# Block 1: six gate tiles of each input projection multiplied inside the attention, and the keys over 512 turned in a second pass

## The reference, cut to what matters

```python
h  = modulate(rms_norm(x,  norm1_g[l]), sh1, sc1)       # latent, 512 tokens
hc = modulate(rms_norm(xc, norm1_g[l]), csh1, csc1)     # context, 256 tokens
qa, ka, va, qb, kb, vb, ga, gb = split_in_proj(h @ w_in[l])
qac, kac, vac, qbc, kbc, vbc, gac, gbc = split_in_proj(hc @ w_in[l])
ya = window_attention_latent(...)   # 128 near keys each way + 256 context keys, with a sink
yb = full_attention_latent(...)     # all 512 + 256 = 768 keys
m  = sigmoid(ga) * (ya @ w_pa) + sigmoid(gb) * (yb @ w_pb)
x  = x + gt1 * (m @ w_o)
```

## Time and profile before

| | |
|---|---|
| median of 3 runs | 3453.82 us (3453.39 to 3454.66) |
| the profiled execution | 3448.93 us |
| its span, first to last instruction | 3447.0 us |
| PE busy | 3302.1 us, 96% |
| DVE, ACT, POOL busy | 51%, 35%, 13% |
| mean granted clock of PE | 0.991 |

### The profile page before, as it was taken

The page is one execution under the profiler, slowest core; times in us unless marked ns, Lnnn a source line. Parts: engine busy times, 40 slices in busy tenths (PEclk is TensorE's granted clock), DMA queues, the critical chain, the costliest instruction groups (busy, mean ns, idle before and its releaser), DMA issues. The chain is left out here.

```text
span 3447.0 us, 49601 instructions
## 1 busy us (share of the span) xinstructions
PE 3302.1 (96%) x20432; PEld 2649.0 (77%) x20432; DVE 1772.4 (51%) x2736; ACT 1203.7 (35%) x2054; POOL 446.6 (13%) x477
## 2 busy tenths in 40 slices
PE   6999999999999999999999999999999998899998
PEld 4887778788888787776887877667888777578886
DVE  5875657664232456655323357654443385744433
ACT  3214762321131222763223333353332333532322
POOL 0211112000000021104500133120000022200000
PEclk9999999999999999999999999999999999999999
DMA  6420013354111121012222221012222220122222
GB/s 243 147 99 19 2 56 135 135 183 141 62 68 68 58 83 68 2 50 93 94 92 97 99 86 56 26 49 92 92 94 103 98 86 3 38 91 92 98 98 80
DMA packets 78265, 290.66 MB, mean 84 GB/s; under 512 B 8672, under 2 KB 9056, under 8 KB 77280
## 3 DMA queue, kind: packets, MB, share of 16 engines
q1 hardware_dynamic: 78048, 287.55, 23.6%
HBM read 285.42 MB, written 2.10 MB: 83 GB/s over the span
## 5 line engine op out<-in xcount | busy, mean ns | idle before, releaser
L459 DVE TENSOR_TENSOR w_low<-ring,w_high 128x1024 fp32r<-128x1024 f32 x418 | 526.9, 1261 | 1348.9 <-ACT w_high L456 1348.2
L494 PE MATMUL ps<-arena_r,w_high 128*128 128x512 f32 x3568 | 1146.1, 386 | 11.2 <-PEq L1517 9.2
L456 ACT ACTIVATE w_high<-ring 128x1024 fp32r<-128x1024 f32 x418 | 442.8, 1060 | 1516.0 <-PE ps L494 1506.9
L494 PEld LDWEIGHTS ps<-arena_r,w_high 128*128 128x128 f32 x3568 | 647.4, 188 | 162.8 <-issue 14.1
L494 PE MATMUL ps<-low,w_high 128*128 128x512 f32 (+1 forms) x2448 | 764.1, 361 | 0.0
L494 PE MATMUL ps<-high,w_high 128*128 128x512 f32 x2368 | 736.4, 361 | 16.2 <-DVE low L992 8.1
L494 PE MATMUL ps<-high,w_low 128*128 128x512 f32 x2368 | 730.8, 359 | 0.0
L494 PE MATMUL ps<-arena_r,w_low 128*128 128x512 f32 (+1 forms) x1456 | 546.5, 388 | 0.0
L494 PEld LDWEIGHTS ps<-high,w_high 128*128 128x128 f32 x2368 | 394.9, 188 | 96.4 <-issue 12.2
L494 PEld LDWEIGHTS ps<-low,w_high 128*128 128x128 f32 x2448 | 411.4, 189 | 74.6 <-issue 0.2
L494 PEld LDWEIGHTS ps<-high,w_low 128*128 128x128 f32 x2368 | 394.9, 188 | 70.4 <-issue 1.0
(11 more groups left out here) (353 smaller groups left out, 2902.5 us busy)
## 6 DMA issues: line engine op xcount, KB each, us to landing
ring<-in_weights SPq DMA_DIRECT2D x428, 512.0 KB, 3.2
arena<-in_ada_rows SPq DMA_DIRECT2D x80, 512.0 KB, 3.9
arena<-in_ada SPq DMA_DIRECT2D x16, 512.0 KB, 15.5
arena<-in_cond_rows SPq DMA_DIRECT2D x3, 1024.0 KB, 5.5
xL<-in_x SPq DMA_DIRECT2D x1, 2048.0 KB, 9.8
out<-xL SPq DMA_DIRECT2D x4, 512.0 KB, 2.7
low_f<-in_low_rank SPq DMA_DIRECT2D x3, 512.0 KB, 4.3
const<-in_const SPq DMA_DIRECT2D x1, 1104.0 KB, 5.2
```

The costliest lines, as they stand in the source:

```text
L456: act.activation(w_high[:, slot, :], ring[:, place, :], ACT.Copy).then_inc(unit_high.sem, 1)
L459: dve.tensor_tensor(w_low[:, slot, :], ring[:, place, :], w_high[:, slot, :].bitcast(F32), ALU.subtract).then_inc(unit_free.sem, 1)
L494: mm = pe.matmul(bank(4 * (t % 2) + 2 * p + s, width), w, g.split[k][s][x], start=(n == 0 and m == 0), stop=(n == len(part) - 1 and m == 2))
```

## The change

Of the 28 tiles of each input projection the last six (gates) are no longer multiplied for the latent tokens there. In layer 0 a third gemm makes these six tiles for the 256 context columns alone; their units come a second time in the weight stream. In both layers a new class `LateGates` multiplies the latent part inside the attention: one tile takes four steps, six of its 24 products in each step, three after the turn and three after the values, from step 1 to step 24, into bank 6. DVE evicts a tile at the next tile's first step; for tiles 2 to 5 POOL makes the high half of the unit and DVE the low half; units 0 and 1 are split at the end of the projection.

To free bank 6, the turned probabilities get one bank for each head (4 and 5), at most 512 keys. What a pair has over 512 keys is turned in a second pass at the start of the step after, ahead of that step's scores, into bank 4, and ACT copies it with one instruction. Each copy now waits for its own head's transposes alone. The halves of `h` stay in use, so probabilities and heads move to other places, and POOL starts to split heads only when the last gate is multiplied. The table of the head work is packed closer. A facility that nothing called (`beside`) is removed.

```diff
+LATE_GATES = (6, 6)
+STEPS_PER_GATE, GATES_FROM = 4, 1
...
-            normed = {6: Z_KB, 9: Z_QB, 12: Z_QB + 1, 15: Z_QB + 2, 18: Z_QB + 3}
-            turned = {2: Z_KA, 5: Z_QA, 7: Z_QA + 1, 9: Z_QA + 2, 11: Z_QA + 3, 13: Z_KB,
-                      15: Z_QB, 18: Z_QB + 1, 21: Z_QB + 2, 24: Z_QB + 3}
+            normed = {6: Z_KB, 9: Z_QB, 11: Z_QB + 1, 13: Z_QB + 2, 15: Z_QB + 3}
+            turned = {2: Z_KA, 5: Z_QA, 7: Z_QA + 1, 9: Z_QA + 2, 11: Z_QA + 3, 12: Z_KB,
+                      14: Z_QB, 16: Z_QB + 1, 18: Z_QB + 2, 20: Z_QB + 3}
...
-            for z0, tiles, both in ((Z_KA, 4, True), (Z_QA, 24, l == 0)):
-                g = Gemm(tiles, 4, 1, K8, segments(both))
+            kinds = [(Z_KA, 4, segments(True)), (Z_QA, Z_TILES - Z_QA - late, segments(l == 0))]
+            if l == 0:
+                kinds.append((Z_TILES - late, late, [(1, C)]))
+            for z0, tiles, segs in kinds:
+                g = Gemm(tiles, 4, 1, K8, segs)
...
+            def products(self, pe, i, half):
+                f, step = divmod(i - GATES_FROM, STEPS_PER_GATE)
+                if not 0 <= f < self.count:
+                    return
+                per = 3 * KD // (2 * STEPS_PER_GATE)
+                first = (2 * step + half) * per
+                slot = (stream["split"] + f) % SPLIT
+                if first == 0:
+                    pe.wait_ge(unit_free.sem, stream["used"] + f + 1)
+                    if f:
+                        pe.wait_ge(gate_out.sem, gate_out.at(f))
+                for n in range(first, first + per):
+                    k, m = divmod(n, 3)
+                    w, x = ((w_high, 1), (w_low, 1), (w_high, 2))[m]
+                    mm = pe.matmul(bank(self.BANK_AT), w[:, slot, k * P:k * P + P], self.split[k][0][x],
+                                   start=(n == 0), stop=(n == 3 * KD - 1))
+                if first + per == 3 * KD:
+                    mm.then_inc(split_used.sem, 1)
...
+            def evict(self, dve, i):
+                f, step = divmod(i - GATES_FROM, STEPS_PER_GATE)
+                if step == 0 and 0 < f <= self.count:
+                    dve.wait_ge(split_used.sem, stream["split"] + f)
+                    dve.tensor_copy(z[:, self.tile0 + f - 1, 0:S], bank(self.BANK_AT)).then_inc(gate_out.sem, 1)
...
                     def turn(j):
-                        tiles = pair["keys"] // P
+                        tiles = min(pairs[j]["keys"], BANK) // P
                         for e in range(2):
                             pe.wait_ge(probs_out.sem, probs_out.at(2 * j + e + 1))
                             if j:
-                                pe.wait_ge(turned_out.sem, turned_out.at(2 * j))
+                                pe.wait_ge(turned_out.sem, turned_out.at(2 * j - 1 + e))
+                            if e == 0 and rests(j):
+                                pe.wait_ge(rest_out.sem, rest_out.at(rests(j)))
...
+                    def turn_rest(j):
+                        pe.wait_ge(turned_out.sem, turned_out.at(2 * j + 1))
+                        for e in range(2):
+                            for m in range(rest(j) // P):
+                                to = T_AT * BANK + e * rest(j) + m * P
+                                mm = pe.transpose(ps[:, to:to + P], room(j, e)[:, BANK + m * P:BANK + m * P + P], con("ident"))
+                        mm.then_inc(rest_in.sem, 1)
...
                     for i in range(n + 2):
+                        if 0 <= i - 2 < n and rest(i - 2):
+                            turn_rest(i - 2)
                         for m in begun(i):
                             scores(m)
                         if 0 <= i - 1 < n:
                             turn(i - 1)
-                        for part in beside:
-                            ...
+                        if gates:
+                            gates.products(pe, i, 0)
                         if 0 <= i - 2 < n:
                             values(i - 2)
+                        if gates:
+                            gates.products(pe, i, 1)
...
                     def copy(j, e):
-                        act.wait_ge(turned_in.sem, turned_in.at(2 * j + 2))
+                        act.wait_ge(turned_in.sem, turned_in.at(2 * j + e + 1))
...
                     for i in range(n + 2):          # ACT
+                        if 0 <= i - 2 < n and rest(i - 2):
+                            copy_rest(i - 2)
                         if i < n:
                             exponent(i, 0)
                             exponent(i, 1)
...
-            attention(pairs1(l), HD ** -0.5)
+            attention(pairs1(l), HD ** -0.5, LateGates(l))
```

More of the change, by code:

```diff
@@ L1280, in project @@
                 for g in stage.gemms:
-                    g.beyond, g.done = (0 if stage.last else 2), ()
+                    g.beyond, g.done = (beyond if stage.last else 2), ()
                 if stage.normed:
@@ L1495, in scores_at, with attention, both_rooms, room @@
+        def attention(pairs, scale, gates=None, more=()):
+            n = len(pairs)
+            T_AT, O_AT = 4, 3584 + 384
+            ahead = gates.count if gates else 0
+            def both_rooms(i):
+                if not gates:
+                    return probs[:, i % 3]
+                return few_probs[:, 2 * (i % 3):2 * (i % 3) + 2, :] if pairs[i]["keys"] <= C else many_probs[i % 3]
+            def room(i, e):
+                return both_rooms(i)[:, e, :]
             def scores_at(i, e):
@@ L1512, in begun, with rest, rests @@
                 return range(count(i - 1) if i else 0, count(i)) if i < n else ()
-            def turned_at(i, e):
-                return T_AT + e * pairs[i]["keys"]
+            def rest(i):
+                return max(pairs[i]["keys"] - BANK, 0)
+            def rests(i):
+                return sum(rest(m) > 0 for m in range(i))
             with nc.Block() as block:
@@ L1605, in normalize @@
                         for e in range(2):
-                            p = probs[:, j % 3, e, 0:pair["keys"]]
+                            p = room(j, e)[:, 0:pair["keys"]]
                             dve.tensor_scalar(p, p, st[:, 4 + e:5 + e], None, ALU.mult).then_inc(probs_out.sem, 1)
@@ L1612, in _ @@
                         if i == n:
-                            split_unit(None, dve, 0, 0, None, 0)
-                            split_unit(None, dve, 1, 1, None, 0)
+                            split_unit(None, dve, ahead, ahead, None, 0)
+                            split_unit(None, dve, ahead + 1, ahead + 1, None, 0)
+                        if gates:
+                            gates.evict(dve, i)
                         for m in begun(i):
                             maxima(m)
-                        for part in beside:
-                            part.vector_parts(dve, i)
+                        if gates:
+                            gates.low(dve, i)
                 @block.scalar
@@ L1659, in _ @@
                         if i == n:
-                            split_unit(act, None, 0, 0, None, 0)
+                            if gates:
+                                act.wait_ge(unit_high.sem, stream["split"] + ahead)
+                            split_unit(act, None, ahead, ahead, None, 0)
                         if 0 <= i - 1 < n:
@@ L1682, in _ @@
                         split(*parts)
+                    if gates:
+                        gates.high(pool)
+                        pool.wait_ge(split_used.sem, stream["split"] + ahead)
                     for j, pair in enumerate(pairs):
```

112 lines of the change are left out of this document (68 added, 44 removed).

## The result

The changed kernel takes 3490.64 us (median of 4 runs, 3490.01 to 3493.19), the kernel before 3453.61 beside it (4 runs, 3453.23 to 3454.66): 1.0108 times, 95% interval 1.0091 to 1.0126. It is 37 us slower; the forecast was 3456 and the range ended at 3476.

What follows compares the result with a forecast made beforehand. PE, busy 96% of the span, was taken to bound the kernel, with a chain through ACT and DVE in block 1's attentions. Projections -64.9, attention +69.7, other attentions -3 gave +1.8 us: 3456, range 3433 to 3476.

Steps and rivals of the forecast that it cites:

- The failed step: Projections: closer-packed head work meets modulation rows on DVE in layer 0, +0.9 us (0 to 6); layer 1 has room.
- The saving itself: Projections: six tiles' latent products removed, saving 32.3 us in layer 0 (2.94 us a tile left) and 33.5 in layer 1.
- Third rival: Layer 0's context-only tiles: weight load and product add up, 5.5 us a tile instead of 2.94, +15.4, so 3471; chance 0.04.
- The attention: Block 1's attentions: each step takes the longer of two paths, 43.75 us a period for 34.46; +34.65 and +35.05 a layer.
- The sum of both paths: Block 1's narrow attention steps: if they took both paths added instead of the longer one, the forecast would all be wrong.
- path A: Attention chain through ACT: later turn waits for the first copy, delaying scores; +1.45 us a narrow step, which it sets (21.75).
- First rival: Attention: the later turn hides, only PE's queue counts, 43.16 us a period; -18.7 us, so 3435; chance 0.26.
- Second rival: Attention: each edge between products and another group drains the array, 0.38 us more a step, +17.5, so 3473; chance 0.27.
- path P: Attention, PE's own queue of scores, turns, products and values: sets the wide steps, 22.0 us for four.
- Block 2: Second block's attentions: first copy may start sooner, at most 6.2 us in all; half taken, -3 us.

Runs made afterwards that it cites:

- the table alone: Kernel before with only the head-work table changed (query-tile norms every 2 tiles instead of every 3): 3485.81 us, ratio 1.0098.
- the kernel without stalls: Changed kernel with the old head-work table in layer 0 and two PSUM banks for the norms' sums in layer 1: 3460.15 us, ratio 1.0028.
- the halved turn: Changed kernel without late gates and with the old table, keeping the second turn of keys over 512 and a bank per head: 3498.28 us, ratio 1.0134.
- the own head's copy: Kernel before, pairs up to 512 keys turned into one bank a head, ACT copying the first head once its transposes end: 3445.78 us, ratio 0.9981.
- one unit ahead and no stalls: The kernel without stalls, with one gate unit instead of two split at each projection's end: 3457.68 us, ratio 1.0019.
- the shorter chain: One unit ahead and no stalls, plus keys over 512 turned in the same step behind its first three products, first head copied early: 3448.57 us, ratio 0.9989.
- the six products together: One unit ahead and no stalls, with the step's six products all ahead of the values instead of three on each side: 3453.95 us, ratio 1.0006.
- both at once: One unit ahead and no stalls, with same-step later turn behind all six products and layer 1's last head turned at tile 19: 3436.76 us, ratio 0.9959.

## Why the forecast was wrong

- **The failed step** is "The head work is packed closer ... I add 0.9 us; between 0 and 6. In layer 1 DVE has room." In place of 0.9 and 0 us it measured 19.7 and 18.5 (the table alone), or 34 together by the medians. I costed the closer work as load on DVE and looked for room there, and in layer 1 DVE does have room: without the stall the same table runs with no gap on PE. But the table also moved a wait: the mean product of a norm against the read of the sum before it, from a round apart into the same round. I had even noted that evictions come 4.3 us after their tile in layer 0, and did not ask what on PE waits for DVE's work behind an eviction.
- **A second omission**, the ends of the projections at nothing: +2.0 and +3.1 us. One is the second split unit (taken away: 1.06 us left). The other is POOL's last turn by the profile, which ends last in the kernel after and in three of its variants; no run took it away.
- **The saving itself was right** where no stall hid it: layer 1 gave 32.6 to 33.6 us for 33.5 in the kernel without stalls. Layer 0's short tiles take (274.61 - 262.58) / 4 = 3.0 us, forecast 2.94, from DVE's evictions:

```profile
262.58 0.42 DVE L1340 COPY arena<-ps 128x256 f32<-128x256 f32 x1
...
274.61 0.42 DVE L1340 COPY arena<-ps 128x256 f32<-128x256 f32 x1
```

- **Third rival**, loads and products add up: refuted by these tiles (5.5 expected) and by loads and products both at a distance of 0.12 us. The Trainium skill's page TensorE: Matmul & The Clock Gate, "The mechanism", also names a background weight buffer beside other rows of the array; I had weighed only half its sentence, and these tiles agree with the whole of it. A line further down in that section says that loads overlap only where the rows differ; these tiles disagree with that line.
- **The attention**, two paths and the longer one per step: +35.6 and +34.9 us for 34.65 and 35.05. The sum of both paths does not occur. That the narrow steps came out by path A (21.7 for 21.75 a period) is partly luck: PE's queue alone would have set them at 21.4, where I had 21.16. Path A alone is measured in the halved turn (41.1 a period; the terms gave 41.95).
- **First rival**, the later turn hides: nearly so in steps with products, where it waits 0.43 us at most and is worth 0.3 us a period. It does not hide in the steps without products, where it waits up to 1.81 us and six steps take 31.5 us for 26.2. PE's queue was also longer than the rival had it.
- **Second rival**, edges drain the array: true in part. Where PE's queue binds, a period is 44.1 for 43.16 worked out, +0.12 a step, and a pair of edges less gave 0.08. By the starts of PE's groups in the kernel after, the first three products and their edge take 0.87 us where path P had 0.79, and the second three 0.80 where it had 0.69 and no edge. The wide scores take 1.49 for 1.42, a turn of eight 0.85 for 0.93. The rival needed 0.15 a step to decide and had 0.38, from edges of 0.17 where its own figures (0.39 less 0.233) give 0.16.
- **Block 2**: -3.7 for -3, of which the own head's copy alone gives -3.4. The -3 was half of a bound of 6.2, so its nearness is luck.

With most of the two missed terms taken out (one unit ahead and no stalls) the kernel measures 3457.68, 5.3 us over the kernel before beside it, where +1.8 was forecast. Layer 0's projection is still short there by the wait of its short tiles, and layer 1's gap is still open. The slower rivals' list named edges, loads and sums of paths, none of them in the part that I had passed over in two sentences.

## What to carry to other kernels

Moving work closer together in a software pipeline is not costed by the load of the engines alone: take each wait of the moved instructions and ask in which round its release now falls, and what stands in the queue behind it. Here a wait that fell into its own round cost 4.1 to 5.1 us each time and about 2 more behind it, at the lower clock; a second buffer moved it back by one round and gave 18 us in one layer. When two paths of a step are nearly equal, shortening one bares the other: the shorter chain gave 9 us alone, the six products together 4, both at once 21 (with the head turned a tile earlier).

## What the runs showed of the hardware

- **A stall costs more than its length.** After the 4.4 us without products the two mean products start 0.98 us apart, where it is 0.43 in the kernel before, and the next product is shown for 1.42 us, where one is shown for 0.39 ahead of the stall. Windows of the kernel after, behind the stall and 3.8 us later (the clock is the third figure from the end):

```profile
1302.20:1305.20 3.00, 2.94 (x5) 1.74 (x6) 2.92 (x5) 0.00 (x0) 0.00 (x0) 0.50 0.44 162
1306.00:1310.00 4.00, 4.00 (x19) 3.22 (x18) 0.00 (x0) 0.00 (x0) 2.31 (x2) 1.00 0.00 0
```

PE worked at 1.2 and then again at 2.4 GHz. By the table alone 26.4 us of gaps made 37.3 to 38.2 us of loss in the profiled execution, about 2 us more for each of the six. The Trainium skill, TensorE: Matmul & The Clock Gate, "HAM oscillation — how this bites in real kernels", describes this for waits on DMAs; here a wait on another engine did it.

- **The same instruction beside POOL.** In the kernel after DVE's subtraction of a unit takes 1.20 to 1.23 us in all 377 places where POOL stands idle (1.23 at 276.55). Where POOL works at some time during it, 20 of 47 stay under 1.3 us and the others take up to 2.32 (1.47 at 1299.45, as in the earlier trace rows). POOL's first product of a turn takes 1.28 us where DVE stands idle and 2.33 where DVE works throughout. What decides between the short and the long ones was not tried.
